# Highs-first weight tiles at the second norm, states and taps made earlier, and stick-breaking scores in row pairs, in a two-layer streaming encoder

## The reference

```python
def sb_attend(q, q_pos, k, v):                       # mixer D, 4 heads of 64
    z = jnp.einsum('bqhd,bshd->bhqs', q, k).astype(jnp.float32) * HEAD_DIM ** -0.5
    strict = jnp.arange(n_keys)[None, :] < q_pos[:, None]
    log_keep = jnp.where(strict, jax.nn.log_sigmoid(-z), 0.0)
    later = lax.cumsum(log_keep, axis=3, reverse=True) - log_keep
    weight = jnp.where(strict, jnp.exp(jax.nn.log_sigmoid(z) + later), 0.0)
    return jnp.einsum('bhqs,bshd->bqhd', weight.astype(v.dtype), v)

def conv_ffn(h, w_up, w_conv, b_conv, w_down, prefix):
    up = h @ w_up                                    # 1024 -> 2 * 2816
    ext = jnp.concatenate([prefix.astype(up.dtype), up], axis=1)
    conv = sum of ext[:, j:j + T] * w_conv[j] over j = 0, 1, 2, plus b_conv
    gate, val = jnp.split(conv, 2, axis=-1)
    return (jax.nn.silu(gate) * val) @ w_down, ext[:, T:]
```

## Time and profile before

| | before |
|---|---|
| median of 3 runs | 1137.81 us (1137.68 to 1139.74) |
| profiled execution, time | 1138.62 us |
| profiled execution, span | 1136.8 us, granted clock 0.995 |
| TensorE matmul busy | 1100.3 us, 97% of the span |
| TensorE weight load busy | 1002.5 us, 88% |
| VectorE | 536.5 us, 47% |
| ScalarE | 595.8 us, 52% |
| GpSimd | 692.6 us, 61% |
| DMA | 216.01 MB, mean 190 GB/s |

### The profile page before, as it was taken

How to read it: one execution, slowest core, us unless ns; L and a number is a source line. 1 busy time by engine, 2 the same in 40 slices (tenths; PEclk the granted TensorE clock), 3 DMA queues, 4 the chain that set the end, 5 groups by cost and what they waited for, 6 DMA issues and landing times.

```text
span 1136.8 us, 22999 instructions
## 1 busy us (share of the span) xinstructions
PE 1100.3 (97%) x8300; PEld 1002.5 (88%) x8300; DVE 536.5 (47%) x1303; ACT 595.8 (52%) x1095; POOL 692.6 (61%) x310
## 2 busy tenths in 40 slices
PE   5799999999999999999999999999999999999996
PEld 0787888788899899999999788888899989999996
DVE  2547523446267754442246562345535775444212
ACT  1555534445446665565456444454554676556542
POOL 0455434455467787777878554445556778777782
PEclk9899999999999999999999999999999999999999
DMA  9855646757554354444566555484544435445452
GB/s 359 331 180 202 220 173 230 253 179 268 205 187 165 109 190 163 157 175 151 187 211 250 198 211 213 162 283 162 184 126 138 162 110 193 166 151 180 151 186 80
DMA packets 82111, 216.01 MB, mean 190 GB/s; under 512 B 9241, under 2 KB 29281, under 8 KB 81777
## 3 DMA queue, kind: packets, MB, share of 16 engines
q1 hardware_dynamic: 82032, 214.93, 54.2%
HBM read 209.85 MB, written 5.05 MB: 189 GB/s over the span
## 4 chain that ended last, share of the span: by engine, by line
PE 70%; issue 13%; POOL 9%; DMA 2%; DVE 2%; ACT 2%; SPq 1%; POOLq 0%; DVEq 0%; ACTq 0%
PE ps L680 13%; PE ps L682 13%; PE ps L681 13%; POOL wlo L581 9%; PE ps L706 8%; PE ps L707 7%; PE ps L708 7%; DMA raw<-stream 2%; PE ps L636 2%; SPq L477 1%; POOL ol L599 1%; PE ps L630 1%; ACT whi L1169 1%; DVE work L1629 0%; PE ps L851 0%
## 5 line engine op out<-in xcount | busy, mean ns | idle before, releaser
L581 POOL TENSOR_TENSOR wlo<-raw,whi 128x1024 fp32r<-128x1024 f32 x282 | 674.6, 2397 | 424.9 <-ACT whi L1169 318.6
L706 PE MATMUL ps<-hh,whi 128*128 128x288 f32 x864 | 264.0, 306 | 1.4 <-POOL wlo L581 0.7
L1169 ACT ACTIVATE whi<-raw 128x1024 fp32r<-128x1024 f32 x204 | 213.2, 1052 | 85.0 <-PE ps L682 43.4
L707 PE MATMUL ps<-hl,whi 128*128 128x288 f32 x864 | 256.1, 296 | 0.0
L708 PE MATMUL ps<-hh,wlo 128*128 128x288 f32 x864 | 255.5, 296 | 0.0
L680 PE MATMUL ps<-oh,whi 128*128 128x290 f32 (+1 forms) x816 | 244.2, 299 | 4.9 <-POOL wlo L581 2.5
L682 PE MATMUL ps<-oh,wlo 128*128 128x290 f32 (+1 forms) x816 | 242.8, 298 | 0.0
L681 PE MATMUL ps<-ol,whi 128*128 128x290 f32 (+1 forms) x816 | 242.1, 297 | 0.0
L706 PEld LDWEIGHTS ps<-hh,whi 128*128 128x128 f32 x864 | 162.7, 188 | 39.0 <-issue 34.7
L707 PEld LDWEIGHTS ps<-hl,whi 128*128 128x128 f32 x864 | 163.0, 189 | 0.1
L708 PEld LDWEIGHTS ps<-hh,wlo 128*128 128x128 f32 x864 | 162.8, 188 | 0.0
(11 more groups left out here) (256 smaller groups left out, 1595.9 us busy)
## 6 DMA issues: line engine op xcount, KB each, us to landing
raw<-stream SPq DMA_DIRECT2D x232, 512.0 KB, 4.3
mraw<-stream SPq DMA_DIRECT2D x40, 1024.0 KB
raw<-stream SPq DMA_DIRECT2D x88, 128.0 KB, 5.0
raw<-stream SPq DMA_DIRECT2D x24, 384.0 KB, 5.2
first<-mod_first SPq DMA_DIRECT2D x16, 512.0 KB, 10.9
raw<-stream SPq DMA_DIRECT2D x24, 256.0 KB, 5.4
o_proj<-proj SPq DMA_DIRECT2D x12, 288.0 KB
kvk<-keys_t SPq DMA_DIRECT2D x6, 512.0 KB, 4.3
```

Of the source, the lines that this page charges most:

```text
L581: nc.gpsimd.tensor_tensor(wlo[:, slot, :], raw[:, slot, :], whi[:, slot, :].bitcast(F32), ALU.subtract).then_inc(lo_ready, 1)
L706: mm(out, whi[:, slot, w], high, start=(i == 0), stop=False)
L707: mm(out, whi[:, slot, w], low, start=False, stop=False)
L1169: A(whi[:, slot, :], raw[:, slot, :], ACT.Copy).then_inc(hi_ready, 1)
```

## The change

In mixer D, `d_scores(j)` now makes the scores of heads 2j and 2j+1 together: each product of head 2j (partitions 0 to 63, bank 2) is followed by that of head 2j+1 (partitions 64 to 127, bank 3). The first call stands at step 20, the second at step 26. The transposes move to step 19 and their copies on ScalarE to step 20, and what follows the second pair moves by a step (logarithms, masks, weights, `d_values(1)` at step 32, the outputs at step 33, the load of mixer C's keys one piece later).

At the second norm the four tiles Q_UP+4 to Q_UP+7 run their 16 products with `whi` first, waiting only for `hi_ready`, and then the 8 with `wlo`. GpSimd makes all eight low rows in one go, behind `wlo` of Q_UP+4. The states of the first four tiles are written in `scale_tile`, and ScalarE makes their first taps between the chunks of high rows and splits Q_UP+7 there too. In the loop a piece is split after the tail of a tile, four pieces ahead of it.

```diff
-                    if q == piece_at(31) + 5:
+                    if q == piece_at(32) + 5:
                         sp.wait_ge(d_out, upto(l, d_out))
...
-                q = lows_and_norm(Q_UP + AHEAD, 2, ((2, 0, 3), (1, 3, KT)))
+                q = lows_and_norm(Q_UP + AHEAD, 2, ((2, 0, KT),))
...
-                def d_scores(h):
-
-                    j, r, z = h // 2, 64 * (h % 2), 2 + h % 2
-                    if h >= 2:
-                        pe.wait_ge(wt_ready, upto(l, wt_ready, h - 1))
-                    k, q = proj[r:r + 64, DK + j, :], proj[r:r + 64, DQ + j, :]
-                    mm(ps[:, z, 0:TP], k[:, 0:P], q[:, 0:TP], start=True, stop=True, skip_group_check=True)
-                    mm(ps[:, z, TP:3 * P], k[:, P:TP], q[:, P:TP], start=False, stop=True, skip_group_check=True)
+                def d_scores(j):
+
+                    if j:
+                        pe.wait_ge(wt_ready, upto(l, wt_ready, 2))
+                    k, q = proj[:, DK + j, :], proj[:, DQ + j, :]
+                    pair = ((2, slice(0, 64)), (3, slice(64, P)))
+                    kw = dict(stop=True, skip_group_check=True)
+                    for z, r in pair:
+                        mm(ps[:, z, 0:TP], k[r, 0:P], q[r, 0:TP], start=True, **kw)
+                    for z, r in pair:
+                        mm(ps[:, z, TP:3 * P], k[r, P:TP], q[r, P:TP], start=False, **kw)
                     for b in range(4):
-                        i = mm(ps[:, z, 3 * P + b * TS:3 * P + (b + 1) * TS], kvk[r:r + 64, j, b * P:(b + 1) * P],
-                               q[:, TP:T], start=False, stop=True, skip_group_check=True)
-                    i.then_inc(z_ready, 1)
+                        for z, r in pair:
+                            i = mm(ps[:, z, 3 * P + b * TS:3 * P + (b + 1) * TS], kvk[r, j, b * P:(b + 1) * P],
+                                   q[r, TP:T], start=False, **kw)
+                            if b == 3:
+                                i.then_inc(z_ready, 1)
...
-                    if t == 20:
-                        pe.wait_ge(kv_d_loaded, upto(l, kv_d_loaded))
+                    if t == 19:
                         pe.wait_ge(scored, upto(l, scored))
...
                         turn_rows(DV, 3, v_turned)
+                    if t == 20:
+                        pe.wait_ge(kv_d_loaded, upto(l, kv_d_loaded))
+                        pe.wait_ge(v_tok, upto(l, v_tok, 1))
                         d_scores(0)
...
-                        d_scores(2)
                     if t == 26:
+                        d_scores(1)
                         d_values(0)
-                        d_scores(3)
-                    if t in (28, 29):
-                        d_log_weights(t - 26)
-                    if t == 31:
+                    if t in (29, 30):
+                        d_log_weights(t - 27)
+                    if t == 32:
                         d_values(1)
...
+                def up_highs_first(slot, q, bank, convolved_tiles, ready=None):
+
+                    o = ps[:, bank, 2:2 + CC]
+                    pe.wait_ge(hi_ready, upto(l, hi_ready, q + 1))
+                    if convolved_tiles is not None:
+                        pe.wait_ge(convolved, upto(l, convolved, convolved_tiles))
+                    for k, high, low in up_terms:
+                        if ready is not None:
+                            pe.wait_ge(ready, upto(l, ready, KT + k + 1))
+                        mm(o, whi[:, slot, k * P:(k + 1) * P], high, start=(k == 0), stop=False)
+                        mm(o, whi[:, slot, k * P:(k + 1) * P], low, start=False, stop=False)
+                    pe.wait_ge(lo_ready, upto(l, lo_ready, q + 1))
+                    for k, high, low in up_terms:
+                        i = mm(o, wlo[:, slot, k * P:(k + 1) * P], high, start=False, stop=(k == KT - 1))
+                    i.then_inc(piece_done, 1)
...
-                for j in range(3):
-                    shift_up(j)
-                    high(Q_UP + AHEAD + 1 + j)
-                    norm_high(2, *UP_CHUNKS[j])
...
+                for j in range(3):
+                    shift_up(j)
+                    high(Q_UP + RING + j)
+                    norm_high(2, *UP_CHUNKS[j])
+                    if j:
+                        up_tile(0, 0, j - 1, None)
+                up_tile(1, 1, 0, None)
+                shift_up(3)
+                high(Q_UP + RING + 3)
+                up_tile(1, 1, 1, None)
+                silu(0, 0)
+                product_high(0, 0)
...
-                    if r is not None:
-                        q = Q_UP + 2 * odd + 4 + g + AHEAD
-                        high_in_loop(r, q, done(q - RING), RING)
...
                     A(tail[:, at(g * FT)], ends, ACT.Copy).then_inc(tap_ready, 1)
+                    if r is not None:
+                        q = Q_UP + 2 * odd + 4 + g + RING
+                        high_in_loop(r, q, done(q - RING), RING)
...
                     if scale is None:
-                        V.tensor_copy(shifts[:, j, :], gap)
+                        in_order(V.tensor_copy(shifts[:, j, :], gap))
+                        st = V_ST + 2 * (j % 2) * FT + j // 2 * 2
+                        V.tensor_copy(gap, vec[:, st:st + 2]).then_inc(state_in, 1)
```

More of the change, by code:

```diff
@@ L1051, in _ @@
                         i.then_inc(znew_ready, 1)
-                        d_scores(1)
                     if t == 23:
@@ L1109, in _ @@
                 pe.wait_ge(pads_ready, upto(l, pads_ready, 2))
+                def up_highs_first(slot, q, bank, convolved_tiles, ready=None):
[12 more added lines that the diff above has]
+                    i.then_inc(piece_done, 1)
                 for j in range(4):
-                    up_piece(slot_for(l, Q_UP + j), Q_UP + 4 + j, UPB + j, j + 1 if j >= 2 else None, hl_ready if j == 0 else None)
+                    up_highs_first(slot_for(l, Q_UP + j), Q_UP + 4 + j, UPB + j, j + 1 if j >= 2 else None, hl_ready if j == 0 else None)
                 with pe.Fori(0, 2 * FT // 4 - 2) as r:
@@ L1395, in _ @@
                         rows_out(3, v_tok)
+                    if t == 21:
                         z_soft_log(0)
@@ L1406, in _ @@
                         z_weights(1)
-                    if t in (26, 27):
-                        z_soft_log(t - 24)
-                    if t in (29, 30):
-                        z_weights(t - 27)
-                    if t == 32:
+                    if t in (27, 28):
+                        z_soft_log(t - 25)
+                    if t in (30, 31):
+                        z_weights(t - 28)
+                    if t == 33:
                         for j in range(2):
@@ L1449, in shift_up, with up_pair @@
                     i.then_inc(up_shifted, 1)
-                for j in range(3):
-                    shift_up(j)
-                    high(Q_UP + AHEAD + 1 + j)
-                    norm_high(2, *UP_CHUNKS[j])
-                def up_pair(p, odd, r=None):
+                def up_pair(p, odd, r):
                     up_tile(p, odd, 0, r)
-                    if r is None and p == 0:
-                        shift_up(3)
-                    if r is not None or p >= 1:
-                        silu(p - 1, 1 - odd)
+                    silu(p - 1, 1 - odd)
                     up_tile(p, odd, 1, r)
-                    if r is not None or p >= 1:
-                        product_high(p - 1, 1 - odd)
+                    product_high(p - 1, 1 - odd)
                 def up_tile(p, odd, g, r):
                     u = 2 * odd + g
-                    if r is not None:
-                        q = Q_UP + 2 * odd + 4 + g + AHEAD
-                        high_in_loop(r, q, done(q - RING), RING)
                     at = (lambda base: bass.ds(p + base, 1)) if not isinstance(p, int) else \
@@ L1479, in up_tile @@
                         act.wait_ge(product_ready, upto(l, product_ready, p - 1))
+                    if r is None:
+                        act.wait_ge(up_shifted, upto(l, up_shifted, 2 * p + g + 1))
                     act.wait_ge(state_in, upto(l, state_in, p * 2 + (g + 1)))
@@ L1982, in _ @@
                         rotate(4)
-                    if t == 26:
+                    if t == 27:
                         mask_z(2)
-                    if t == 27:
                         mask_z(3)
-                        keep(2)
                         rotate(5)
                     if t == 28:
+                        keep(2)
+                        choose(1, 1)
+                    if t == 29:
                         keep(3)
-                        choose(1, 1)
                     if t == 29:
@@ L2044, in convolve @@
                     up = ps[:, up_bank(u) if isinstance(p, int) and p == 0 else UPB + u, :]
-                    if isinstance(p, int) and 2 * p + g < NU:
-                        dve.wait_ge(up_shifted, upto(l, up_shifted, 2 * p + g + 1))
-                    else:
```

(5 more changed lines are left out.)

8 lines of the change are left out of this document (3 added, 5 removed).

## The result

| | before | after |
|---|---|---|
| median on one chip | 1138.38 us (4 runs, 1137.68 to 1139.74) | 1129.25 us (4 runs, 1128.1 to 1130.78) |
| profiled execution: time, span | 1138.62, 1136.8 | 1129.87, 1128.1 |
| mean granted clock in it | 0.995 | 0.989 |

A forecast was written before the change was run, and what follows sets the result against it. TensorE's own time was taken to bound the kernel, with some waits at the second norm. Savings of 6.6 and 3.6 us made 10.2, from the median of 1137.81 to 1127.6, range 1126.0 to 1129.8 (1125.4 to 1131.6 with rivals).

The forecast's parts named there:

- Scores in row pairs: Mixer D: a pair of heads costs what one head did, 1.66 us, saving 3.3 a layer, 6.6 in all.
- Rival A: Mixer D: only wide products overlap, narrow passes gain nothing; 6.8 us saved in all, 1131.0; chance 0.09.
- rival D: Mixer D: pairs do not overlap at all, serialised by banks or weight loads; 1134.2 us; chance 0.03.
- The cover at step 20: Mixer D: copies of the transposes finish 0.8 us before TensorE needs them, so no wait.
- The second norm: Four tiles from Q_UP+4 end at 396.7 instead of 398.50, saving 1.8 us a layer, 3.6 in all.
- 10 x 0.134: Second norm, first tile: ten products left after the last low row, 0.134 us each, so it ends at 387.05.
- three tiles at 3.21 follow: Second norm: the tiles after the first run without waits, 9.65 us, ending at 396.7.
- the sum: Whole kernel: 6.6 us from mixer D plus 3.6 from the second norm, 10.2 saved.
- step 43: Mixers, steps 43 and on: stalls should not change by a microsecond, else the prediction is wrong.
- The loop: Up tiles: work only moved, costed at nothing while VectorE and ScalarE stay below 3.21 us a tile.
- rival C: Loop: the moved split lengthens the chain to 3.67 us a tile, 0.46 over TensorE's; about 1153; chance 0.04.

The follow-up runs named there:

- e1: Kernel before with the mixer D part alone (scores in row pairs, moved steps), second norm as before: 1131.76 us, ratio 0.9938.
- f3: Changed kernel with GpSimd's old order of low rows (0 to 2, `wlo` of Q_UP+5, then 3 to 7): 1130.88 us, 0.9924 of the kernel before.
- f4: Changed kernel with TensorE's old order, three products a step, in all four second-norm tiles: 1132.3 us, 0.9934 of the kernel before.
- f1: Changed kernel, unedited, run again on a second chip: 1130.11 us, 0.9916 of the kernel before.
- g1: Changed kernel, unedited, run again on a third chip: 1129.47 us, 0.9916 of the kernel before.
- f2: Changed kernel with eight unneeded products where TensorE waits for the sixth low row: 1127.91 us, 0.9891 of the kernel before.
- e4: Changed kernel with the first of the four second-norm tiles back at three products a step: 1128.17 us, 0.990 of the kernel before.
- g4: Changed kernel with three products a step in the first second-norm tile, repeated on the third chip: 1127.95 us, 0.9901 of the kernel before.

## Why the prediction was right

**Scores in row pairs: right, a little small.** 1.67 us a pair for 1.66, and 3.51 a layer for 3.3; e1 alone gave 7.1 of 6.6. The choice that mattered was to take the eight narrow passes as riding along like the wide ones, although no row showed narrow passes with full weights. Sixteen of them take 0.98 and eight 0.97. Rival A (only wide products overlap: near 2.6 a pair) and rival D (3.3) fall on that one line. The Trainium skill, "TensorEngine Tiling (Array Packing)", Overview, promises up to 2x for contractions of 64 or less; the trace agrees, with 1.99 (2 x 1.66 for 1.67), and the same page's Instruction Overhead, weighed for rival A, did not bind here. The cover at step 20 was 1.0 in layer 0 and 1.0 in layer 1 for the forecast 0.8, and no wait appeared.

**The second norm: right in its mechanism and in layer 1 to 0.05, wrong in layer 0.** The last low row came at 385.46 for 385.5, state copies cost 0.27 for 0.26, the second tile of layer 1 starts 0.38 later than before for the forecast 0.45, and four tiles take 15.35 for 15.4. Waits for `wlo` and for the convolution are gone. f3 and f4 show that both orders count, each losing 0.8 to 1.0 a layer when taken back.

**The step that failed** is "10 x 0.134" and with it "three tiles at 3.21 follow": they price every product at the full clock. The wait of 1.3 us ahead of these products is in the working itself. The sixth low row comes at 383.9 and TensorE is ready for it at 381.32 + 5 x 0.27 = 382.65. I counted the wait as lost time, and not as a change in what follows. In the profiled execution the half clock made 1.8 + 1.8 into 0.31 + 1.85. The prediction listed no such rival. That the median came out so near the forecast is in part luck, as the misses have opposite signs: with the wait filled the median is 1.5 and 2.2 lower on two chips, 11.2 and 12.4 below the kernel before there, which is more than the 10.2 of the sum. Of that surplus the trace shows 0.2 a layer for the pairs and 0.37 at step 43; the rest was not traced.

**The smaller terms.** The loop was costed at nothing, and in layer 0 it is: 36 tiles take 116.28 us in both kernels, to the hundredth, so rival C's 0.46 a tile is nowhere. In layer 1 they take 116.74 in this profile, 0.46 more. Of that 0.11 lie in the first tile (3.34), ahead of which ScalarE waits for a piece of weights; the other 35 take 3.24 on average instead of 3.23, and why is open. In f1 the 36 take 116.39 and in g1 and f2 116.28. In the stretch of the mixers the engine next after TensorE is ScalarE with 19.15 us, not GpSimd with 17.68 as the prediction reads it; nothing hung on that. Step 43 gave 0.3 in layer 0, and in layer 1 its gap is anything from under 0.6 to 2.1 us in the profiles of this study.

**Of the two orders for the first tile**, the prediction saw that the new one makes it end later (+0.45). It did not ask why the first tile should have it at all. e4 and g4 show that it needn't, and that undoing it there gives a kernel at 1128.0 to 1128.2 (0.990 of before twice), 1.5 below the change on the one chip that had both. With the fillers it is 1127.9 to 1128.0. These two are the fastest versions, equal within what the runs can tell.

## What to carry to other kernels

Products that use different row halves of the array cost as much in pairs as alone, even narrow ones, if they are issued alternately, here always into different banks; one behind the other they overlap at the seam alone. When an edit gathers short waits into a longer one, price what follows at both clock levels (here 1.5 us behind 1.3 of waiting). If the wait can't be shortened, try giving TensorE something harmless to do in it: that paid here, on two chips, though the reason isn't settled. An earlier start of a stretch is only worth as much as the lead of the loads behind it: in layer 1 of e4 and g4 the 0.9 us gained in the first tile went to a piece that hadn't landed.

## What the runs showed of the hardware that was not expected

- A clock at 0.50 for 3.4 us in the middle of a kernel that is otherwise at full clock from 41 to 1122 us, behind waits of 1.33, 0.65 and 0.52 between products. It came in 3 of 14 such places and cost 1.5 us in both profiles of the changed kernel that had it (16.87 and 16.85 us for four tiles instead of 15.35), and 0.8 in f3, where the tile still waits for low rows meanwhile (17.00 in layer 0, 16.16 in layer 1).
- Products issued one head behind the other overlap by 0.53 us at the seam (2.79 for two heads, 1.66 for one).
- Sixteen narrow products of 32 columns in row pairs last 0.98 us, eight on one row half 0.97. So the 0.12 us of one alone buy two, one on each half.
- Eight filler products of 208 columns in a wait of 1.33 us cost nothing measurable, and make the time less by 1.5 to 2.2 us in the median.
